# One streaming encoder step on one core: a root per token tile, token tiles first in the load queue, gate rows spread later, slot-weight sums in a gap

## The chip, the cores and the metric

The kernel runs on one core of a Trainium2 chip. The metric is the device time of one execution in microseconds, median of three runs. The core has five engines with a queue of instructions each: TensorE (PE, with its weight loads as PEld), VectorE (DVE), ScalarE (ACT), GpSimd (POOL) and SyncE (SP). Any of SP, ACT and POOL can issue DMA transfers. Engines wait for each other on semaphores.

## The reference

One layer of a hybrid encoder, for 512 prompt tokens and 8 x 16 sample tokens (640 tokens in all, width 1024):

```
mod = silu(c) @ w_ada + b_ada                        # shift, scale, gate; twice, per request
h   = rms_norm(x, norm1_g) * (1 + sc1) + sh1
q, k, v, indexer, stick-breaking q/k/v, gate logits = split(h @ w_in)
o_a = attention over the top-k keys that an indexer picks
o_b = stick-breaking attention (per-frame causal, in log space)
merged = sigmoid(gl_a) * (o_a @ w_branch_a) + sigmoid(gl_b) * (o_b @ w_branch_b)
x   = x + g1 * (merged @ w_out)
h   = rms_norm(x, norm2_g) * (1 + sc2) + sh2
x   = x + g2 * moe(h)      # 16 experts in 4 groups, top 2 of one group, weights normalised
```

All data are float32. New keys and values are outputs too.

## The kernel before, in words

Every engine's program is written out by hand, in order, with semaphores between them; nothing reorders it. The 640 tokens are five tiles of 128 (`NT`, the fifth holds the samples). SBUF is one tensor `mem` cut by hand.

Weights come in slabs of 2 MB through four rotating buffers. SP issues them in a fixed order (L646 to L663) and reuses a buffer when PE has counted `slab_used` up. The first slabs are ada 0, ada 2, the qa columns of `w_in`, and ada 1; near the merge they are the two halves of the gate columns, `w_branch_a` (two transfers), `w_branch_b`, and then two more gate halves (L663).

The head. SP issues eight small loads (condition vectors, `const_f` with the identity and eps, bias and norm rows, L635 to L643), then the five token tiles (L645), then slabs. ACT takes Silu of the conditions (L819), squares each token tile with a running sum (L831), and takes one root over the sums of all tiles (L833). PE turns the Silu result (L1602) and spreads the small rows (L1608 to L1614); VectorE copies these rows out (L1117 to L1120), waits for `h_sums`, takes one reciprocal (L1124), and then for each tile scales it (L1129) into one of two buffers `ht`; PE turns it (L1595), and ACT and VectorE each copy half of the result. ACT's squares have used the same two buffers `ht` as a place to write. After the fifth tile PE does the ada products (L1625) of slabs 0 and 2, the rows are turned (L1636), ACT and VectorE modulate, and PE starts the qa projection (L1677).

The merge. For 16 units PE makes two gate products (L1996) and two branch products (L2007), always two units' gates and then two units' branches. ACT takes sigmoids (L1039), VectorE multiplies (L1397), and POOL adds the two (L747). Ahead of its 16 additions POOL waits until the last attention unit is done (`bv_done`) and spreads the gate, shift and scale rows of the second half of the layer from a DRAM table over the partitions: two calls of `spread` (L742, L743), each one transfer for the prompt and eight for the samples. VectorE waits for them only in the residual (L1403).

Into the experts. VectorE computes the router's choice, ranks the 1280 token entries into slots of 64-row units, and gives PE one-hot matrices. PE multiplies them into slot tokens (L2081); VectorE turns these into row numbers (`slots_ready`, L1531), for which POOL waits to gather the first rows (L774). VectorE then sums each token's two affinities (L1533 to L1536), normalises them, and builds the matrix for PE's second product, the slot weights (L2088), which PE does before it turns the first gathered rows. The expert loop follows.

Of the kernel before, what the change touches and what calls it, by code (L numbers as in the profile page):

```python
# [29 lines left out]
ALU = mybir.AluOpType  # L30
ACT = mybir.ActivationFunctionType
X = mybir.AxisListType.X

P = 128
D = 1024
# [6 lines left out]
HD = 64  # L42
# [22 lines left out]
NCOND = 1 + DEC_B  # L65
# [12 lines left out]
O_CF = O_H + 5120  # L78
NCF = 5 * 128 + 16 + 16 + 2 * UNITS + 4 * NT + 4 + 16
# [4 lines left out]
O_TMP = O_ST + 180  # L84
# [54 lines left out]
def build(nc, a, o, scratch):  # L139

    ctx = ExitStack()
    with ctx:
# [6 lines left out]
        def view(at, n, pat=None, **dims):  # L149
            v = mem[:, at:at + n]  # L150
            return v if pat is None else v.rearrange(pat, **dims)
# [20 lines left out]
        xt = view(O_F, 5120, "p (t n) -> p t n", t=NT)  # L172
# [18 lines left out]
        eps = view(O_CF + 544 + UNITS, 1)  # L191
        at = O_CF + 545 + UNITS
# [18 lines left out]
        ssum = view(st, NT); rstd = view(st + 5, NT)  # L211
# [11 lines left out]
        rows_t = view(O_OB + 2 * P, P)  # L223
# [4 lines left out]
        s9T = view(O_OA + 1280 + 28 * P, KD * 32, "p (k n) -> p k n", k=KD)  # L228
        assert 1280 + 28 * P + KD * 32 <= 5120
        ht = [view(O_TMP + 1024 * i, 1024) for i in range(2)]  # L230
        c9 = view(O_TMP + 6144, 1024)[0:NCOND]
        s9 = view(O_TMP + 7168, 1024)[0:NCOND]

# [38 lines left out]
        g1 = {False: view(O_TMP, 1024), True: view(O_TMP + 1024, 1024)}  # L272
        bc2 = {False: view(O_TMP + 2048, 2048), True: view(O_TMP + 4096, 2048)}
# [28 lines left out]
        aw = [view(rt + 30 + 5 * i, 5) for i in range(2)]  # L302
        den = view(rt + 40, 5); rden = view(rt + 45, 5)
# [319 lines left out]
        def spread(eng, dst, lo, n, s, s_prompt=None):  # L623

            eng.dma_start(dst[False], modd[0:1, lo:lo + n].broadcast_to([P, n])).then_inc(s_prompt or s, 16)
            for b in range(DEC_B):
                eng.dma_start(dst[True][DEC_S * b:DEC_S * b + DEC_S, :],
                              modd[1 + b:2 + b, lo:lo + n].broadcast_to([DEC_S, n])).then_inc(s, 16)
# [3 lines left out]

        @block.sync
        def _(sp):
            sp.dma_start(c9[0:1, :], a["c_prompt"]).then_inc(c9_ld, 16)  # L635
            sp.dma_start(c9[1:NCOND, :], a["c_sample"]).then_inc(c9_ld, 16)
            sp.dma_start(view(O_CF, NCF), a["const_f"]).then_inc(c_ld, 16)
            for n_, at in (("b_ada", 0), ("norm1_g", 48), ("norm2_g", 56)):
                row = a[n_].rearrange("a (r n) -> (a r) n", n=P)
                sp.dma_start(rows_t[at:at + row.shape[0]], row).then_inc(rows_ld, 16)  # L640
            sp.wait_ge(rows_zero, 1)
            for i, n_ in enumerate(("qn_g", "kn_g")):
                sp.dma_start(rows_t[64 + i:65 + i, 0:HD], a[n_]).then_inc(rows_ld, 16)  # L643
            for t in range(NT):
                sp.dma_start(xt[:, t, :], xs if t == SMP else xp[P * t:P * t + P, :]).then_inc(tile_ld[t], 16)  # L645
            for n, s in enumerate(slabs):  # L646
                if n >= NSLAB:
                    sp.wait_ge(slab_used, n - NSLAB + 1)
                for dst, src in slab_moves(s, n):
                    sp.dma_start(dst, src).then_inc(slab_ld[n % NSLAB], 16)  # L650
                if s == ("b", XB - 1):

                    sp.wait_ge(av_done, NA)
                    for w, n_ in enumerate(("cache_b_k", "cache_b_v")):
                        sp.dma_start(xb[w], a[n_][0, XB].rearrange("(c p) h d -> p c (h d)", p=P)).then_inc(xb_ld, 16)
                if n == NSLAB:
                    sp.dma_start(view(O_CB, NCB // 2), a["const_b"]).then_inc(cb_ld, 16)
                if s == ("brb",):

                    sp.wait_ge(bv_done, NB)  # L660
                    sp.wait_ge(rows_st, 160)
                    for g in range(2):
                        sp.dma_start(gx[g], by_k(w_in, COL["gl"] + D * g + 512, 512)).then_inc(gx_ld[g], 16)  # L663

            def expert_part(e, w):

                k = 3 * (e % 3) + w
                src = a[("w_exp_gate", "w_exp_up", "w_exp_down")[w]][0, e].rearrange("(k p) n -> p k n", p=P)
                sp.dma_start(mw[k].rearrange("p (k n) -> p k n", k=4 if w == 2 else KD), src).then_inc(w_ld[k], 16)


            sp.wait_ge(merge_read, 1)
            for w in range(3):
                expert_part(0, w)
            expert_part(1, 0)
            sp.wait_ge(wo_done, 1)
            expert_part(1, 1)
            expert_part(1, 2)
            expert_part(2, 0)
            sp.wait_ge(e_in, 1)  # L680
            expert_part(2, 1)
            sp.wait_ge(slots_ready, 1)
            sp.wait_ge(h2_st[0], 48)
            sp.wait_ge(h2_st[1], 32)
            sp.wait_ge(hx_ld, 16)
            sp.wait_ge(unit_w_ready, 1)
            expert_part(2, 2)
            for e in range(3, NE):
                for w, part_used in enumerate((gate_used, up_used, down_used)):
                    sp.wait_ge(part_used, e - 2)  # L690
                    expert_part(e, w)

            sp.wait_ge(y_all, 1)
            for t in range(NT):
                sp.dma_start(ysum[t], yd[P * t:P * t + P, :]).then_inc(tile_ld[t], 16)
            for t in range(NT):
                sp.wait_ge(e_out, 100 + t + 1)
                sp.dma_start(out_rows("y", t), ysum[t]).then_inc(out_st, 16)
            sp.wait_ge(out_st, 16 * NT)
# [3 lines left out]
        def _(pool):  # L703
            own = Own(pool, pool_did)
# [12 lines left out]
            for t in range(NT):  # L717
                pool.wait_ge(ro_ready, t + 1)
                if t == 0:
                    pool.wait_ge(zeros_ready, 1)  # L720
                    for r_ in range(0, TOK + UNIT, P):
                        n_ = min(P, TOK + UNIT - r_)
# [16 lines left out]
            pool.wait_ge(m9_st[1], 64)  # L739

            pool.wait_ge(bv_done, NB)
            spread(pool, g1, 2048, 1024, bc2_ld)  # L742
            spread(pool, bc2, 3072, 2048, bc2_ld)  # L743
            for i in range(16):
                m, h = i // 2, i % 2
                pool.wait_ge(gb_ready, i + 1)
                g.tensor_tensor(mergedT[:, m, 320 * h:320 * h + 320], gb[i % 2][0], gb[i % 2][1],  # L747
                                ALU.add).then_inc(merged, 1)
            pool.wait_ge(merge_read, 1)
# [31 lines left out]
            for e in range(NE):  # L781
                n = g.value_load(unit_n[0:1, e:e + 1], min_val=1, max_val=TOK // UNIT)
                at = g.value_load(unit_0[0:1, e:e + 1], min_val=0, max_val=UNITS - 1)
# [20 lines left out]
        def _(act):  # L804
            own = Own(act, act_did)
            s = nc.scalar
# [6 lines left out]
            def copy_out(key, dst, src=None, scale=1.0):  # L813
                r = result(act, key)
                ins = s.activation(dst, r if src is None else src, ACT.Copy, scale=scale)
                return ins

            act.wait_ge(c9_ld, 32)
            s.activation(s9, c9, ACT.Silu).then_inc(s9_ready, 1)  # L819
            act.wait_ge(c_ld, 16)  # L820
# [7 lines left out]

            for t in range(NT):
                act.wait_ge(tile_ld[t], 16)  # L830
                own(s.activation(ht[t % 2], xt[:, t, :], ACT.Square, accum_out=ssum[:, t:t + 1]))  # L831
                own.settle()
            s.activation(rstd, ssum, ACT.Sqrt, scale=1.0 / D, bias=eps).then_inc(h_sums, 1)  # L833
            for t in range(NT):
                r = result(act, ("h1T", t, 0))
                read(("h1T", t, 0), s.activation(hT[:, 0:4, P * t:P * t + P],
# [15 lines left out]
            for t in range(NT):  # L852
                r = result(act, ("qa", t))
                read(("qa", t), s.activation(tok[:, t, 0:512], r, ACT.Copy))
            for t in range(NT):
                r = result(act, ("kvq", t))
# [242 lines left out]
        def _(dve):  # L1099
# [3 lines left out]
            def step(ins):  # L1103
                own(ins)
                own.settle()
# [14 lines left out]
            own(v.tensor_copy(g9, r[:, 2 * P:4 * P].rearrange("p (i n) -> p i n", i=2)))  # L1120
            own.settle()
            dve.sem_inc(free[place["rows"][0]], 1)
            dve.wait_ge(h_sums, 1)
            step(v.reciprocal(rstd, rstd))  # L1124
            for t in range(NT + 1):
                if t < NT:
                    if t >= 2:
                        result(dve, ("h1T", t - 2, 1))
                    v.tensor_scalar(ht[t % 2], xt[:, t, :], rstd[:, t:t + 1], None, ALU.mult).then_inc(h_ready, 1)  # L1129
                if t >= 1:  # L1130
                    r = result(dve, ("h1T", t - 1, 1))
                    read(("h1T", t - 1, 1), v.tensor_copy(hT[:, 4:8, P * (t - 1):P * t], r.rearrange("p (k q) -> p k q", k=4)))
# [385 lines left out]
            own(v.tensor_tensor(at_pos_b, bcast(iota_p, [P, 2 * NT, P], 1), bcast(entry_pos, [P, 2 * NT, P], 2), ALU.is_equal))  # L1518
            own.settle()
            dve.sem_inc(entries_ready, 1)  # L1520

            r = result(dve, "slots")[:, 0:3 * UNITS].rearrange("p (a j) -> p a j", a=3)
            own(v.memset(ids[:, UNITS:UNITS + 2, :], 0))
# [6 lines left out]
            step(v.tensor_scalar(ids[:, 0:UNITS, 1], dest, -1.0, row_half, ALU.mult, ALU.add))  # L1530
            dve.sem_inc(slots_ready, 1)  # L1531

            for i, oh in enumerate((oh1, oh2)):  # L1533
                step(v.tensor_tensor(t2, aff, oh, ALU.mult))
                step(v.tensor_reduce(aw[i], t2, X, ALU.add))
            step(v.tensor_tensor(den, aw[0], aw[1], ALU.add))  # L1536
            step(v.reciprocal(rden, den))
            for i in range(2):
                own(v.tensor_tensor(ew[:, :, i], aw[i], rden, ALU.mult))
# [640 lines left out]
```

## Time and profile before

| | |
|---|---|
| median of 3 runs | 1188.93 us (1186.75 to 1189.68) |
| profiled execution | 1187.63 us, its span 1185.8 us |
| PE busy | 1068.2 us, 90% of the span |
| VectorE, ACT, POOL busy | 389.4, 244.0, 143.5 us |
| mean granted clock of PE | 0.96 of full speed |
| DMA | 217.05 MB, mean 183 GB/s |

The span is the time from the first to the last instruction of one execution; the rest of the execution's time lies around it. The chain of waits is followed back from the last instruction: each piece is what released the next. A wait of an engine off that chain costs nothing. The granted clock is a share of 2.4 GHz; 0.50 is the lower level.

### The profile page before, as it was taken

Reading aid. Unit: us, or ns where it says so; the run is one execution under the profiler, and the core shown is the slowest. Engines: PE = TensorE matmul, PEld = TensorE weight load, DVE = VectorE, ACT = ScalarE, POOL = GpSimd, SP = SyncE. Lnnn points to the kernel's source line nnn. Section 1 sums busy time; section 2 is a strip of 40 time slices with the busy share of each in tenths; the row PEclk is TensorE's granted clock in tenths of the full one; section 3 lists DMA queues with packets and bytes.
Section 4 is the critical chain, followed back from the end, with each engine's and each line's share of the span. In section 5 each row is a group of like instructions: output and inputs, shape, how many; then the busy total and the mean of one; then the engine's idle time right before and its main releaser. Section 6 shows DMA issues by size and latency. Waiting matters only on the chain.

```text
span 1185.8 us, 21577 instructions
## 1 busy us (share of the span) xinstructions
PE 1068.2 (90%) x8635; PEld 714.0 (60%) x8635; DVE 389.4 (33%) x894; ACT 244.0 (21%) x486; POOL 143.5 (12%) x218
## 2 busy tenths in 40 slices
PE   5899999989979979889999999955999999999991
PEld 4445764456745757667677754425676767677770
DVE  2100738956777655200000003353111111111114
ACT  4111232127745335200000001121111101010100
POOL 0000210110000000200000010010222222222221
PEclk9999999999979989999999999976999999999996
DMA  9542855345000248880030027066796996999935
GB/s 344 221 149 88 311 170 189 110 122 193 1 1 1 72 144 283 231 232 1 19 123 1 1 99 293 36 220 223 256 305 204 358 366 215 316 381 373 382 93 195
DMA packets 103029, 217.05 MB, mean 183 GB/s; under 512 B 9477, under 2 KB 17749, under 8 KB 102694
## 3 DMA queue, kind: packets, MB, share of 16 engines
q1 hardware_dynamic: 91446, 184.42, 43.5%
q0 software_dynamic: 11504, 31.52, 9.8%
q8 instruction: 55, 0.90, 0.3%
q14 instruction: 24, 0.20, 0.1%
HBM read 196.87 MB, written 19.05 MB: 182 GB/s over the span
## 4 chain that ended last, share of the span: by engine, by line
PE 79%; DVE 8%; DMA 5%; ACT 4%; issue 3%; SPq 0%; DVEq 0%; POOL 0%; ACTq 0%; POOLq 0%
PE ps L2105 17%; PE ps L1996 10%; PE ps L1651 10%; PE ps L2116 9%; PE ps L2007 6%; PE ps L2051 4%; PE ps L1677 3%; PE ps L1696 3%; PE ps L1595 3%; PE ps L1625 2%; DMA mem<-in_w_branch_b 2%; DMA mem<-in_x_sample 2%; PE ps L1778 2%; PE ps L2110 1%; ACT mem L952 1%
## 5 line engine op out<-in xcount | busy, mean ns | idle before, releaser
L2105 PEld LDWEIGHTS ps<-mem 128*64 128x64 f32 x3584 | 198.5, 138 | 24.8 <-issue 21.4
L2105 PE MATMUL ps<-mem 128*64 128x128 f32 x3584 | 209.5, 275 | 2.1 <-DVE mem L1552 0.9
L1996 PE MATMUL ps<-mem 128*128 128x320 f32 x512 | 139.2, 433 | 1.1 <-DVEq L1359 1.1
L1996 PEld LDWEIGHTS ps<-mem 128*128 128x128 f32 x512 | 97.3, 190 | 41.5 <-issue 1.3
L1651 PE MATMUL ps<-mem 128*128 128x512 f32 (+1 forms) x320 | 113.3, 514 | 1.8 <-ACT mem L912 0.9
L2116 PE MATMUL ps<-mem 128*64 128x512 f32 x448 | 107.1, 597 | 4.2 <-DVE mem L1566 0.5
L1651 PEld LDWEIGHTS ps<-mem 128*128 128x128 f32 x320 | 54.2, 191 | 58.5 <-issue 58.5
L1595 PE MATMUL ps<-mem 128*128 128x128 f32 x432 | 66.9, 294 | 22.8 <-DVE mem L1129 8.8
L1397 DVE TENSOR_TENSOR mem<-mem,ps 128x320 f32<-128x320 f32 x32 | 15.6, 488 | 198.1 <-PE ps L2007 198.1
L1564 DVE TENSOR_TENSOR mem<-mem,ps 128x128 f32<-128x128 f32 x56 | 16.1, 288 | 186.9 <-PE ps L2105 186.9
L1595 PEld LDWEIGHTS ps<-mem 128*128 128x128 f32 x432 | 53.4, 151 | 36.7 <-DVE mem L1129 9.8
L2007 PE MATMUL ps<-mem 128*128 128x320 f32 x256 | 72.2, 441 | 3.5 <-DMA mem<-in_w_branch_b 3.4
L2051 PE MATMUL ps<-mem 128*128 128x512 f32 x160 | 72.3, 608 | 2.1 <-POOL mem L747 2.1
L2007 PEld LDWEIGHTS ps<-mem 128*128 128x128 f32 x256 | 49.5, 194 | 25.1 <-DMA mem<-in_w_branch_b 3.9
L1093 ACT ACTIVATE mem<-ps,mem 128x512 f32<-128x512 f32 x28 | 19.2, 687 | 185.5 <-PE ps L2116 185.5
L2116 PEld LDWEIGHTS ps<-mem 128*64 128x64 f32 x448 | 31.2, 136 | 40.4 <-issue 40.4
L2051 PEld LDWEIGHTS ps<-mem 128*128 128x128 f32 x160 | 30.4, 194 | 38.7 <-issue 38.7
L1039 ACT ACTIVATE mem<-ps 128x320 f32<-128x320 f32 x32 | 14.0, 437 | 191.1 <-PE ps L1996 191.1
L1566 DVE COPY mem<-ps 128x128 f32<-128x128 f32 x56 | 16.3, 292 | 95.2 <-PE ps L2110 95.2
L791 POOL DMA_INDIRECT expert_rows<-mem x28 | 44.6, 1595 | 23.3 <-POOL mem L789 23.3
L1214 DVE MAX8 mem<-mem 128x8 f32<-128x644 f32 (+3 forms) x65 | 41.0, 631 | 2.0
L1215 DVE MATCH_REPLACE8 mem<-mem 128x644 f32<-128x644 f32 (+3 forms) x65 | 39.9, 613 | 0.0
(288 smaller groups left out, 1141.3 us busy)
## 6 DMA issues: line engine op xcount, KB each, us to landing
mem<-in_w_exp_gate SPq DMA_DIRECT2D x16, 2048.0 KB, 12.5
mem<-in_w_exp_up SPq DMA_DIRECT2D x16, 2048.0 KB, 17.9
mem<-in_w_exp_down SPq DMA_DIRECT2D x16, 2048.0 KB, 22.3
mem<-in_w_ada SPq DMA_DIRECT2D x12, 2048.0 KB, 14.4
mem<-in_w_in SPq DMA_DIRECT2D x9, 2048.0 KB, 13.1
mem<-in_cache_b_k SPq DMA_DIRECT2D x8, 1024.0 KB, 5.6
mem<-in_cache_b_v SPq DMA_DIRECT2D x8, 1024.0 KB, 8.5
mem<-in_w_out SPq DMA_DIRECT2D x2, 2048.0 KB, 11.4
```

Source lines behind the costliest of these rows:

```text
L791: pool.indirect_dma_start(y_halves, bass.IndirectOffsetOnAxis(ap=idx_out, axis=0), yj, None, compute_op=ALU.add).then_inc(y_st, 16)
L1214: step(v.max(top8, sc))
L1215: step(v.match_replace(sc, top8, sc, TAKEN))
L1595: last = tr(dst[:, P * k:P * k + P], b, ident)
L1651: last = mm(b[:, 0:w], hT[:, k, P * t:P * t + P], slab_k[n][:, k, 0:w], start=(k == 0), stop=(k == KD - 1))
L1677: last = mm(b, hT[:, k, P * t:P * t + P], slab_k[n_qa][:, k, :], start=(k == 0), stop=(k == KD - 1))
L1696: last = mm(b[:, 0:320], slab_k[n][:, k, P * m:P * m + P], hT[:, k, 320 * h:320 * h + 320], start=(k == 0), stop=(k == KD - 1))
L1996: last = mm(b[:, 0:320], w[:, k, P * (m % 4):P * (m % 4) + P], hT[:, k, 320 * h:320 * h + 320], start=(k == 0), stop=(k == KD - 1))
L2007: last = mm(b[:, 0:320], slab_4[slab_no[s_] % NSLAB][:, k, P * m:P * m + P], rows_of[:, k, 320 * h:320 * h + 320], start=(k == 0), stop=(k ...
L2051: last = mm(b, mergedT[:, k, P * t:P * t + P], slab_k[sn][:, k, :], start=(k == 0), stop=(k == KD - 1))
L2105: last = mm(b[UNIT * h:UNIT * h + UNIT, 0:P], x_, w[:, k, 256 * h + P * c:256 * h + P * c + P], start=(k == 0), stop=(k == KD - 1), skip_g ...
L2116: last = mm(bank(7)[UNIT * n:UNIT * n + UNIT, :], hidT[c][:, UNIT * h:UNIT * h + UNIT], w[:, 2 * h + c, 512 * n:512 * n + 512], start=(c = ...
```

## The change

Four edits. (1) The eight small loads move from SP's queue to the beginning of ACT's; the token tiles are now SP's first issues. (2) The norm's root and reciprocal are done for each tile by itself, and the squares go to two buffers of their own. (3) POOL issues the two `spread` calls inside its addition loop, after the second unit's products are ready and ahead of the second addition. (4) The five VectorE instructions that sum the slot weights move ahead of VectorE's wait for PE's slot product.

```diff
@@ first norm's buffers
         ht = [view(O_TMP + 1024 * i, 1024) for i in range(2)]
+        sq_first = [view(O_TMP + 2048 + 1024 * i, 1024) for i in range(2)]
@@ SP
-            sp.dma_start(c9[0:1, :], a["c_prompt"]).then_inc(c9_ld, 16)
-            sp.dma_start(c9[1:NCOND, :], a["c_sample"]).then_inc(c9_ld, 16)
-            sp.dma_start(view(O_CF, NCF), a["const_f"]).then_inc(c_ld, 16)
-            for n_, at in (("b_ada", 0), ("norm1_g", 48), ("norm2_g", 56)):
-                row = a[n_].rearrange("a (r n) -> (a r) n", n=P)
-                sp.dma_start(rows_t[at:at + row.shape[0]], row).then_inc(rows_ld, 16)
-            sp.wait_ge(rows_zero, 1)
-            for i, n_ in enumerate(("qn_g", "kn_g")):
-                sp.dma_start(rows_t[64 + i:65 + i, 0:HD], a[n_]).then_inc(rows_ld, 16)
             for t in range(NT):
                 sp.dma_start(xt[:, t, :], ...).then_inc(tile_ld[t], 16)
@@ POOL
             pool.wait_ge(bv_done, NB)
-            spread(pool, g1, 2048, 1024, bc2_ld)
-            spread(pool, bc2, 3072, 2048, bc2_ld)
             for i in range(16):
                 m, h = i // 2, i % 2
                 pool.wait_ge(gb_ready, i + 1)
+                if i == 1:
+                    spread(pool, g1, 2048, 1024, bc2_ld)
+                    spread(pool, bc2, 3072, 2048, bc2_ld)
                 g.tensor_tensor(mergedT[:, m, 320 * h:320 * h + 320], gb[i % 2][0], gb[i % 2][1],
                                 ALU.add).then_inc(merged, 1)
@@ ACT
+            (the eight loads and the wait for rows_zero, as they stood on SP, now act.dma_start)
             act.wait_ge(c9_ld, 32)
             s.activation(s9, c9, ACT.Silu).then_inc(s9_ready, 1)
...
             for t in range(NT):
                 act.wait_ge(tile_ld[t], 16)
-                own(s.activation(ht[t % 2], xt[:, t, :], ACT.Square, accum_out=ssum[:, t:t + 1]))
+                own(s.activation(sq_first[t % 2], xt[:, t, :], ACT.Square, accum_out=ssum[:, t:t + 1]))
                 own.settle()
-            s.activation(rstd, ssum, ACT.Sqrt, scale=1.0 / D, bias=eps).then_inc(h_sums, 1)
+                s.activation(rstd[:, t:t + 1], ssum[:, t:t + 1], ACT.Sqrt, scale=1.0 / D, bias=eps).then_inc(h_sums, 1)
@@ VectorE, first norm
-            dve.wait_ge(h_sums, 1)
-            step(v.reciprocal(rstd, rstd))
             for t in range(NT + 1):
                 if t < NT:
+                    dve.wait_ge(h_sums, t + 1)
+                    step(v.reciprocal(rstd[:, t:t + 1], rstd[:, t:t + 1]))
                     if t >= 2:
                         result(dve, ("h1T", t - 2, 1))
@@ VectorE, slots
             dve.sem_inc(entries_ready, 1)
+            for i, oh in enumerate((oh1, oh2)):
+                step(v.tensor_tensor(t2, aff, oh, ALU.mult))
+                step(v.tensor_reduce(aw[i], t2, X, ALU.add))
+            step(v.tensor_tensor(den, aw[0], aw[1], ALU.add))
 
             r = result(dve, "slots")[:, 0:3 * UNITS].rearrange("p (a j) -> p a j", a=3)
...
             dve.sem_inc(slots_ready, 1)
 
-            for i, oh in enumerate((oh1, oh2)):
-                step(v.tensor_tensor(t2, aff, oh, ALU.mult))
-                step(v.tensor_reduce(aw[i], t2, X, ALU.add))
-            step(v.tensor_tensor(den, aw[0], aw[1], ALU.add))
             step(v.reciprocal(rden, den))
```

## Rows read from the trace of the kernel before

**Rows 1.** The page: engines' shares of the chain that ended last.

```profile
PE 79%; DVE 8%; DMA 5%; ACT 4%; issue 3%; SPq 0%; DVEq 0%; POOL 0%; ACTq 0%; POOLq 0%
```

**Rows 2.** Timeline of the merge's beginning: start, us, engine, line, operation, [idle before].

```profile
482.94 1.37 SPq L650 DMA_DIRECT2D mem<-in_w_branch_a  x2
...
512.17 8.42 PE L2007 MATMUL ps<-mem 128*128 128x320 f32 x24 [3.36 <-DMA mem<-in_w_branch_b]
```

**Rows 3.** Chain of waits in the merge: start, us, what.

```profile
487.33 24.80 DMA mem<-in_w_branch_b
...
615.73 8.61 PE ps L2007 x32
```

**Rows 4.** Transfers by line: branch A (L650), the spread (L627), one gate half alone.

```profile
DMA to landing us min/median/max: 8.5/10.9/13.2
...
L627 POOL DMA_DIRECT2D mem<-mod_rows x16: 484/486/547, 488.4 to 496.2; - x16
...
DMA to landing us min/median/max: 11.0/16.1/23.6
...
DMA to landing us min/median/max: 8.8/8.8/8.8
```

**Rows 5.** Timeline of the head, columns as in rows 2.

```profile
0.74 1.28 ACT L819 ACT_TABLE_LOAD   x1 [0.74 <-PEq L2166]
...
3.03 1.05 ACT L819 ACTIVATE mem<-mem 9x1024 f32<-9x1024 f32 x1 [1.01 <-DMA mem<-in_c_sample]
...
3.64 1.93 SPq L645 DMA_DIRECT2D mem<-in_x_prompt  x4
5.04 1.02 PE L1602 MATMUL ps<-mem 9*128 9x9 f32 x8 [5.04 <-DMA mem<-in_const_f]
...
8.51 1.06 ACT L831 ACTIVATE mem<-mem 128x1024 f32<-128x1024 f32 x1 [4.42 <-DMA mem<-in_x_prompt]
...
10.05 0.42 DVE L1120 COPY mem<-ps 128x256 f32<-128x256 f32 x1
...
16.39 0.19 DVE L1124 RECIPROCAL mem<-mem 128x5 f32<-128x5 f32 x1 [5.92 <-ACT mem L833]
```

**Rows 6.** Chain of waits in the head, columns as in rows 3.

```profile
24.89 2.15 PE ps L1625 x72
...
27.33 2.21 PE ps L1625 x72
...
33.81 8.80 PE ps L1677 x16
...
44.72 7.06 PE ps L1677 x16
```

**Rows 7.** Two slab loads of the head: durations in ns, start, and landing.

```profile
L650 SPq DMA_DIRECT2D mem<-in_w_ada x1: 3157/3157/3157, 7.0 to 7.0; - x1
L650 SPq DMA_DIRECT2D mem<-in_w_in x1: 5126/5126/5126, 10.2 to 10.2; - x1
...
DMA to landing us min/median/max: 17.3/19.2/21.0
```

**Rows 8.** Windows: us, engines' busy time, PE's granted clock, DMA share, GB/s.

```profile
1.50:6.50 5.00, 1.02 (x8) 0.92 (x8) 0.23 (x1) 1.58 (x2) 1.50 (x2) 1.00 0.80 261
...
512.10:516.60 4.50, 4.42 (x10) 2.93 (x11) 0.45 (x1) 0.00 (x0) 0.00 (x0) 0.62 1.07 165
```

**Rows 9.** Timeline on the way into the experts, columns as in rows 2.

```profile
809.72 0.19 DVE L1524 COPY mem<-ps 128x36 f32<-128x36 f32 x1 [1.24 <-issue]
...
811.23 0.25 DVE L1534 TENSOR_TENSOR mem<-mem 128x80 f32<-128x80 f32 x1
...
812.53 0.19 DVE L1537 RECIPROCAL mem<-mem 128x5 f32<-128x5 f32 x1
...
813.67 4.48 PE L2088 MATMUL ps<-mem 128*128 128x36 f32 x20 [4.00 <-DVEq L1543]
```

**Rows 10.** SP's own waits from 780 to 820: line, releaser, us, times, longest.

```profile
SPq L686 <- DVE mem L1545: 2.6, 1, 2.6
```

More of the change, by code:

```diff
@@ L816, in copy_out @@
                 return ins
+            act.dma_start(c9[0:1, :], a["c_prompt"]).then_inc(c9_ld, 16)
+            act.dma_start(c9[1:NCOND, :], a["c_sample"]).then_inc(c9_ld, 16)
+            act.dma_start(view(O_CF, NCF), a["const_f"]).then_inc(c_ld, 16)
+            for n_, at in (("b_ada", 0), ("norm1_g", 48), ("norm2_g", 56)):
+                row = a[n_].rearrange("a (r n) -> (a r) n", n=P)
+                act.dma_start(rows_t[at:at + row.shape[0]], row).then_inc(rows_ld, 16)
+            act.wait_ge(rows_zero, 1)
+            for i, n_ in enumerate(("qn_g", "kn_g")):
+                act.dma_start(rows_t[64 + i:65 + i, 0:HD], a[n_]).then_inc(rows_ld, 16)
             act.wait_ge(c9_ld, 32)
```

## The prediction

> **What bounds the kernel now.** I read the page first, then the chain of waits over the whole span, then timelines, waits and landings of the three stretches that the change touches. The chain lies on PE for 79% of the span [rows 1], so a stage before or between PE's work is worth exactly what PE waits there, and what PE then loses at half clock. SP's slab loads, POOL's row stores and the later stages are started by PE's progress, so time won early is carried to the end unless a transfer is late in its turn.
>
> Stretch one, the head. PE's main work begins with the qa projection at 33.81 us [rows 6]. It hangs on: token tiles landed, one root for all five, a reciprocal at 16.39, five scale-and-transpose rounds that end at 24.89, two ada slabs on PE (the second from 27.33), modulation [rows 5, 6]. Stretch two, the merge. After branch A's first eight products PE stands 3.36 us, until 512.17, for branch B's weights, which landed 24.80 us after their issue at 487.33 [rows 2, 3]; when it goes on, the granted clock is 0.62 over 4.5 us [rows 8], which is mostly the lower of the two levels (1.2 against 2.4 GHz). Stretch three, the way into the experts: PE waits 4.00 us for VectorE before the slot-weight product at 813.67, and VectorE itself had stood 1.24 us just before 809.72 [rows 9].
>
> **The change part by part.**
>
> *Gate rows later (merge).* POOL issues 18 transfers, two large ones and sixteen small ones that start 488.4 to 496.2, 0.49 us each; together they are about 3.1 MB by their shapes, and they landed 11.0 to 23.6 us after issue [rows 4]. So they lie exactly beside SP's branch weights. Without them the queue holds branch A (2 MB, second half landed by 482.94 + 1.37 + 13.2 = 497.5 at the latest, though part of that was beside the spread [rows 2, 4]) and branch B behind it. A 2 MB slab issued with nothing beside it landed in 8.8 us [rows 4], so branch B lands by 497.5 + 8.8 = 506.3. PE wants it at 512.17 - 3.36 = 508.8. Lower bound of the gain 0 (B as late as now), upper bound the whole wait, 3.36; I take all of it. Then the clock: after the wait 24 products took 8.42 us, where a full set of 32 takes 8.61 [rows 3], that is 6.46 for 24; 1.96 us were lost at the low level. With no wait ahead of it I count that back too (bounds 0 and 1.96). Sum -5.3 us.
> What the move adds: POOL now waits for the second gated product, issues the 18 (18 x 0.49, about 9 us) and only then makes its second addition. Queued behind it: VectorE's fourth gated product waits for that addition. But PE first makes gates 2 and 3, 64 products, twice the 32 of [rows 3] and so some 17 us, so about 8 us are spare. The spread lands some 25 us after 516, while the rows are read after the merge, near 718; SP asks for no slab in that time except the gate halves, issued before. Cost 0; if POOL took over 17 us, each further one would show as PE waiting in the fourth branch product.
>
> *Sums of the slot weights.* Five small VectorE instructions, 811.23 to 812.53 = 1.30 us [rows 9], leave the path ahead of weights_ready and go into the 1.24 us in which VectorE waits for PE's slot product. They overrun it by about 0.15 us (settling included), which delays slots_ready by as much. Gain 1.30 - 0.15 = 1.15 us, with 0.9 and 1.3 as bounds. What is late next: the gather of the first expert rows, which would be 0.15 us later; SP, which waits for it and then for the slot weights, still waited 2.6 us for the latter [rows 10], so after 1.15 + 0.15 us it is still 1.3 us early. PE's 4.5 us product stays last. -1.15 us.
>
> *Head.* First the constants. Eight small issues go from SP to ACT. ACT issued none before, so their price there is not shown: on SP they are what lies between the engines' first instructions at 0.74 and the first tile at 3.64, 2.9 us in all [rows 5]; POOL's cost 0.49 to 0.55 each [rows 4], which would make 4 to 4.4. I take SP's, as the same kind of queue. The table load (1.28, at 0.74 until now hidden) and the Silu (1.05) come behind them: Silu ends at 3.64 + 1.28 + 1.05 = 5.97 instead of 4.08. const_f is issued as early as before, but beside the tiles: I take 6.0 us for PE's first transposes instead of 5.04 [rows 5] (bounds 5.97 from Silu, and 13.5, when all five tiles had landed until now). VectorE's row copies ended at 10.05 + 0.42 = 10.47, 5.43 after that start; now 11.4.
> Then the norm. VectorE no longer waits for the root of all tiles (till 16.39) and starts at 11.4. From 16.39 to 24.89 it and PE took 8.50 us for five rounds with one reciprocal; four more at 0.22 make 9.4, so the transposes end at 20.8, 4.1 us earlier. ACT hides behind that: Square from about 6.0 (tile 0, 2.9 us earlier than the 8.51 shown, is there), 1.15 each, then a table load 1.28 once (taken from the norm's single one) and a root a tile. Even at 1 us each, which is far above the 0.19 of the reciprocal of the same size, the roots end at about 9.4, 11.6, 13.7, 15.9 and 18.0, and VectorE asks for them at 11.4, 12.4, 15.2, 17 and 18.7. Without that cover each us by which ACT is late goes into the sum. The squares go to a buffer of their own, so the scaled tiles are not waited for.
> Then the slabs, which decide how much of the 4.1 arrives. The second ada slab landed 7.0 + 17.3 = 24.3, qa's 10.2 + 21.0 = 31.2 [rows 7]. SP's issues come 2.9 us earlier, but the bytes ahead of them are the same, moved from one queue to another, and the DMA engines were already busy 0.80 of the time from 1.5 to 6.5 [rows 8]: only 1 us of idle to be won, of which part is the start. I take 0.7: 23.6 and 30.5. PE comes to the second ada at 20.8 + 2.5 = 23.3, starts at 23.6, and by the 6.48 us from 27.33 to 33.81 would begin qa at 30.1; the slab holds it till about 30.4. Gain 3.4 us; bounds 2.6 (slabs no earlier) and 4.1 (slabs never wait).
> A rule of the Trainium skill bears on this: DMA: Bandwidth & Descriptors, section "Issuing engines are not separate DMA queues", says that transfers started by different engines run on the same 16 DMA engines and interleave, so that several issuers save only the issue time. The trace agrees: POOL's and SP's transfers of [rows 3, 4] lay beside each other and took up to 24.80 us each. By the rule the head gives 3.4; if queues were independent, 4.1.
> Clock in the head: qa's first sixteen products took 8.80 us where the next sixteen took 7.06 [rows 6], so 1.7 us are lost after PE's pause before 33.81. That pause stays, a little longer, and I leave the loss as it is; bounds -1.7 (it goes) and +1.7 (it doubles).
>
> **Sum.** 3.4 + 5.3 + 1.15 = 9.85 us. The profiled execution took 1187.63 us (span 1185.8 and 1.8 around it): 1177.8. The median of the three runs shown lies 1.3 above it; half of that added gives 1178.5 for the time after.
>
> **Rivals.**
> *The head gives nothing, or costs a little.* The constants on ACT's queue reach PE later than 6.0: the transposes end 14.8 us after const_f (6.0 to 20.8), so from a landing at 10.1 on nothing of the root's gain is left, and at 12 the head costs 1.9. For it: the tiles now have the first places, and const_f is the only large piece among the constants. Against it: POOL's first transfer, issued behind SP's branch slabs and gate halves, landed in 11.0 us [rows 4], so two queues do share. Total 1181 to 1183.
> *Constants starve behind everything SP has queued.* This is the one that ends slower. If const_f came only after the tiles and the two ada slabs, at 23.6, transposes would end at 38.4, 13.5 later than now; against 6.45 won elsewhere that is +7: 1194 to 1195. It decides from a landing at 16.6 on. What speaks for it is only that branch B took 24.80 us beside another queue; that was half the rate, not starvation.
> *The merge wait stays.* If branch A's odd layout and not the spread is what delays branch B, or if it is the gate halves behind it, only the head and the tail count: 1187.63 - 4.55 + 0.65 = 1183.7. Against: both queues were full from 488 to 512, and 3.1 MB of that were the spread's.
> *More than the sum.* The head's low-clock stretch goes as well, or the slabs never hold PE: 1176 to 1177, both 1174 to 1175.
>
> **How the numbers follow.** Forecast (7 to 12 us won, own range 1175.5 to 1182) 0.70; head without gain 0.14; merge wait stays 0.06; starving 0.03; more than 12 us won 0.07. The range 1174.5 to 1184 takes the forecast and the cases without head or merge gain. What a measurement here can tell from no change is about 0.3%, 3.6 us: faster 0.93 (nearly all of the first three and the last), same 0.04 (two rivals at once), slower 0.03.
>
> **What would show it.** Right: no wait of PE for branch B near 505 and no stretch at 0.62 there; branch B landing within 20 us of issue; POOL's 18 issues near 510 and no PE wait at the fourth branch product; VectorE's first scale near 12, transposes ended near 21, the qa products starting near 30.4 with the qa slab as the last to come; VectorE busy through the slot product, and PE's wait before the slot weights 2.9 us instead of 4.00. Wrong: PE's first transposes after 10 us; a second table load among the roots; a new low-clock stretch; the same span between 34 and 487 of before not found again.

## The result, and the profile after

The changed kernel took 1183.04 us (median of 5 runs, 1180.37 to 1183.4) against 1188.06 for the kernel before: measured ratio 0.9945, 95% interval 0.9927 to 0.9964 (it is not the quotient of the two medians, 0.9958). A second set, the fifth run below, gave 1180.4 us, 0.9935 (0.992 to 0.995). The profiled execution took 1183.28 us, its span 1181.5. So it is faster by 5 to 8 us where 9.85 were forecast, and the time lies inside the range, 4.5 us above the point.

**The head won next to nothing.** Timeline of the head after; ACTq and SPq are issues of transfers.

```profile
0.74 0.53 ACTq L811 DMA_DIRECT2D mem<-in_c_prompt  x1
0.74 1.81 SPq L637 DMA_DIRECT2D mem<-in_x_prompt  x4
...
1.63 0.38 ACTq L813 DMA_DIRECT2D mem<-in_const_f  x1
...
3.89 0.32 ACTq L819 DMA_DIRECT2D mem<-in_kn_g  x1
4.24 1.28 ACT L821 ACT_TABLE_LOAD   x1 [4.24 <-issue]
5.53 1.05 ACT L821 ACTIVATE mem<-mem 9x1024 f32<-9x1024 f32 x1
...
9.34 1.06 ACT L833 ACTIVATE mem<-mem 128x1024 f32<-128x1024 f32 x1 [2.75 <-DMA mem<-in_const_f]
9.36 1.02 PE L1604 MATMUL ps<-mem 9*128 9x9 f32 x8 [9.36 <-DMA mem<-in_const_f]
...
11.01 0.45 PE L1610 MATMUL ps<-mem 128*128 128x128 f32 x1 [0.64 <-DMA mem<-in_kn_g]
...
15.08 0.16 DVE L1128 RECIPROCAL mem<-mem 128x1 f32<-128x1 f32 x1
```

const_f was issued at 1.63, hardly later than before (1.49), but PE had it only at 9.36 instead of 5.04 [rows 5]; the last small row held PE until 11.01. VectorE's copies of those rows ended at 14.9 instead of 10.47, so that its first reciprocal came at 15.08 and its first scale at 15.28. The rest is in the chain of waits:

```profile
3.89 6.99 DMA mem<-in_kn_g
...
24.33 2.15 PE ps L1627 x72
26.47 0.29 issue
26.76 2.21 PE ps L1627 x72
...
33.24 9.69 PE ps L1679 x16
...
45.03 7.06 PE ps L1679 x16
```

Transposes end at 24.33 instead of 24.89, qa begins at 33.24 instead of 33.81 [rows 6]: 0.57 us won. Its first sixteen products took 9.69 us instead of 8.80, since the low level of the clock began ahead of them this time (0.50 already from 32 to 33 us, where the kernel before has 1.00). So at qa's second half the kernel is 0.3 us behind.

**The merge won what was forecast.** Chain of waits, then the landing of branch B (issued at 487.28) and of the spread's sixteen small transfers, then the window that answers to the second of [rows 8].

```profile
489.31 17.47 PE ps L1998 x64
506.77 8.61 PE ps L2009 x32
515.38 17.23 PE ps L1998 x64
```

```profile
DMA to landing us min/median/max: 14.7/14.7/14.7
...
L628 POOL DMA_DIRECT2D mem<-mod_rows x16: 484/484/544, 516.9 to 524.7; - x16
DMA to landing us min/median/max: 2.4/4.5/8.4
```

```profile
512.10:516.60 4.50, 4.50 (x19) 3.15 (x18) 0.98 (x2) 0.00 (x0) 0.92 (x2) 1.00 0.02 5
```

The first 32 branch products run through in 8.61 us at the higher level. Branch B landed 14.7 us after issue, not 24.80 [rows 3], 4.8 us before these products began. From the first gate product to the end of these branches it is 26.07 us. Before it was 31.39, from 489.20 in the timeline to 520.59 in the chain:

```profile
489.20 17.47 PE L1996 MATMUL ps<-mem 128*128 128x320 f32 x64 [1.14 <-DVEq L1359]
...
520.59 17.23 PE ps L1996 x64
```

So 5.3 us, all of it still there when the next pair of units is done: POOL's nine microseconds of issues, from 516, held nobody. By themselves the spread's sixteen small transfers land within 2.4 to 8.4 us; beside SP's they took 11.0 to 23.6 [rows 4].

**The sums won what was forecast.** Timeline on the way into the experts, and SP's own wait:

```profile
804.29 0.24 DVE L1524 TENSOR_TENSOR mem<-mem 128x80 f32<-128x80 f32 x1
...
805.60 0.19 DVE L1530 COPY mem<-ps 128x36 f32<-128x36 f32 x1
...
807.10 0.19 DVE L1539 RECIPROCAL mem<-mem 128x5 f32<-128x5 f32 x1
...
808.25 4.48 PE L2090 MATMUL ps<-mem 128*128 128x36 f32 x20 [2.91 <-DVEq L1545]
```

```profile
SPq L678 <- DVE mem L1547: 1.3, 1, 1.3
```

PE waits 2.91 instead of 4.00 [rows 9], and SP's spare time behind the gather is the 1.3 us that was worked out from [rows 10].

**Two losses between them are in no step of the change.** The residual's load took 15.14 us where it had taken 14.29 (0.85), and the first expert's 96 products 8.17 instead of 7.20 (0.97):

```profile
698.99 15.14 DMA mem<-in_x_sample
...
808.25 4.48 PE ps L2090 x20
...
814.50 8.17 PE ps L2107 x96
```

Head +0.3 (0.57 won, 0.89 to the clock), merge -5.3, sums -1.1, these two +1.8: -4.3, the difference of the spans. The experiments below say which of these are chance.

### The profile page after: what moved, and what is told of

It is laid out like the page before. It is cut to its first block, busy times and chain, and to the rows that moved or that the text cites. A ratio compares the mean times of both kernels' runs of the same rounds, so it can differ in the third digit from the quotient of the medians.

```text
span 1181.5 us, 21581 instructions
## 1 busy us (share of the span) xinstructions
PE 1066.0 (90%) x8630; PEld 713.7 (60%) x8635; DVE 390.2 (33%) x898; ACT 244.7 (21%) x490; POOL 143.6 (12%) x218
## 4 chain that ended last, share of the span: by engine, by line
PE 81%; DVE 8%; ACT 4%; issue 3%; DMA 3%; ACTq 0%; DVEq 0%; POOL 0%; POOLq 0%
PE ps L2107 17%; PE ps L1998 12%; PE ps L1653 10%; PE ps L2118 9%; PE ps L2009 6%; PE ps L2053 4%; PE ps L1679 3%; PE ps L1698 3%; PE ps L1597 3%; PE ps L1627 2%; PE ps L1780 2%; DMA mem<-in_x_sample 1%; PE ps L2112 1%; ACT mem L954 1%; PE ps L1771 1%
## 5 line engine op out<-in xcount | busy, mean ns | idle before, releaser
L1566 DVE TENSOR_TENSOR mem<-mem,ps 128x128 f32<-128x128 f32 x56 | 16.1, 288 | 187.7 <-PE ps L2107 187.7
L740 POOL TENSOR_TENSOR mem<-mem 128x320 f32<-128x320 f32 x16 | 13.7, 858 | 403.5 <-DVEq L1402 403.4
```

## The experiments

The fourth is an edit of the kernel before, the fifth is the changed kernel itself, all others are edits of the changed kernel; each was timed beside the kernel before. Medians of 6 runs (third and fourth: 12, tenth: 5).

**First: constants back on SP, the norm per tile kept.**

```diff
 SP:  +(the eight loads, ahead of the tiles)
 ACT: -(the eight loads)
```

> The changed kernel with the eight constant loads back on SP, ahead of the token tiles. Theory A (the constants on ACT's queue come in behind the tiles, const_f at 9.36 us and the last norm row at 10.9, and that holds the whole head): PE's first transposes again near 5.0 us, VectorE's row copies done near 10.5, the first scale near 11.5, tile transposes ended near 21 instead of 24.3, and qa's products from about 31.2, when their slab lands: 2.0 us earlier than in the changed kernel, some 1181 us, or up to 1 us off that by the clock. Rival B (the reciprocal and the root for each tile are what make the five rounds slow): transposes end at 24 or later, as the tiles come 2.9 us later, and the time is that of the changed kernel or 1 to 2 us above it.

1179.41 us, 0.9913 (0.9895 to 0.9931). PE timeline:

```profile
4.43 1.02 PE L1604 MATMUL ps<-mem 9*128 9x9 f32 x8 [4.43 <-DMA mem<-in_const_f]
...
19.46 2.17 PE L1627 MATMUL ps<-mem 128*32 128x128 f32 x72
...
25.92 4.07 PE L1627 MATMUL ps<-mem 128*32 128x128 f32 x72 [4.29 <-DMA mem<-in_w_ada]
...
34.30 8.16 PE L1679 MATMUL ps<-mem 128*128 128x512 f32 x15 [3.37 <-DVE mem L1151]
```

Rival B falls: with one root and one reciprocal for each tile the transposes are done at 19.5, 5.4 us earlier than in the kernel before. But the gain is gone at the next step: PE stands 4.29 us for the second ada slab, then works at half clock (4.07 us for what takes 2.17), and qa begins at 34.30, no earlier than ever, where 31.2 was expected: this wait had no place in the expectation. The time seemed 3 us below that of the changed kernel, which this profile does not explain; the fifth and sixth runs settle it.

**Second: const_f alone first on SP.**

```diff
 SP:  +sp.dma_start(view(O_CF, NCF), a["const_f"]).then_inc(c_ld, 16)     # ahead of the tiles
 ACT: -act.dma_start(view(O_CF, NCF), a["const_f"]).then_inc(c_ld, 16)
```

> The changed kernel with const_f alone moved from ACT's queue to the first place in SP's; the seven small loads stay on ACT. Theory A: const_f lands near 4.5, the Silu ends near 6.2, PE's first transposes start at about 6.2 instead of 9.36, the small rows no longer stand behind const_f in their queue, transposes end near 21.2, qa's products start near 29.8: 3.4 us under the changed kernel, about 1179.6 us. Rival A2 (not const_f but any load on ACT's queue is late beside SP's tiles, for its place in the queue and not its size): the last norm row is still near 10 us, PE's row products stay near 11, and nothing is won.

1178.32 us, 0.9904 (0.9887 to 0.9921). What PE waited for up to 32 us, and its chain:

```profile
PE ps L1604 <- ACT mem L821: 5.9, 1, 5.9
...
PE ps L1610 <- DMA mem<-in_kn_g: 1.7, 1, 1.7
```

```profile
4.30 19.40 DMA mem<-in_w_ada
23.75 2.21 PE ps L1627 x72
...
30.23 8.74 PE ps L1679 x16
```

const_f landed 3.5 us after its issue, PE starts at 5.9 behind the Silu, and qa begins at 30.23, 3.0 us earlier than in the changed kernel and 0.4 from what was expected. Theory A holds in the trace, with a share for the second rival: the last small row still came 5.4 us after its issue (at 8.5), and PE stood 1.7 us for it. What ends last in this profile is the second ada slab, at 23.7; in the ninth run, the same kernel, it is the last small row. The time is 0.3% to 0.4% under the two sets of the changed kernel, as forecast, though its interval still meets that of the second set (0.992 to 0.995).

**Third: the spread early again.**

```diff
             pool.wait_ge(bv_done, NB)
+            spread(pool, g1, 2048, 1024, bc2_ld)
+            spread(pool, bc2, 3072, 2048, bc2_ld)
```

> The changed kernel with the two spreads of gate rows back ahead of POOL's additions. Theory A: the wait of PE for branch B's weights (3.4 us) and the stretch at half clock behind it (2.0 us) come back, 5.3 us above the changed kernel, about 1188.3 us; PE's merge begins and ends as before the change. Rival C (the merge is held by the gate halves or by branch A's layout, and the gain came from elsewhere): the wait stays away and the time that of the changed kernel.

1188.73 us, 0.9988 (0.9972 to 1.0005). The wait is back (first fence, PE's waits), and the stretch at half clock behind it (second, a window):

```profile
PE ps L2008 <- DMA mem<-in_w_branch_b: 5.2, 1, 5.2
```

```profile
512.20:516.70 4.50, 4.50 (x9) 2.93 (x10) 0.00 (x0) 0.00 (x0) 0.00 (x0) 0.50 0.99 166
```

The merge is worth 0.43% to 0.53% against the two sets of the changed kernel, 5 to 6 us, and rival C falls. The wait is longer than the 3.36 us of before: PE came to its first gate product 1.9 us earlier here (487.35 against 489.20), while branch B landed at 512.15 against 512.13. What PE had won ahead of the merge was lost in the wait, so this run does not say what the head is worth.

**Fourth: the queue move alone, on the kernel before.**

> The kernel before with only the eight loads moved from SP's to ACT's queue; one root for all tiles, spread and sums as before. Theory A: const_f again near 9.4 us, ACT, which needs its eps, starts its squares near 9.4 instead of 8.5, the root ends near 17.3 instead of 16.4, transposes end near 25.8, qa's products start about 0.9 us later than before: 1189 us, no gain at all from tiles that land 3 us earlier. Rival B: the tiles' earlier landing is worth 1 to 3 us by itself, 1185 to 1187.

1190.19 us, 1.0006 (0.9993 to 1.002). PE's timeline, and its chain:

```profile
9.57 1.02 PE L1602 MATMUL ps<-mem 9*128 9x9 f32 x8 [9.57 <-DMA mem<-in_const_f]
...
34.49 8.80 PE ps L1677 x16
```

const_f reached PE at 9.57, qa began at 34.49, 0.7 us later than in the kernel before; in time no change can be told. Tiles that land 1.3 to 3.6 us earlier are worth nothing by themselves.

**Fifth and sixth: the changed kernel and the first experiment's, side by side.**

> The changed kernel itself once more, on the same chip as the next three, to compare with. Theory A (the head of the changed kernel is worth nothing, the merge 5 us, the slot-weight sums 1 us): 0.9945 of the time before, some 1183 us, const_f again at 9.3 to 9.6 us. Its wait for the last load of the residual and its low-clock stretches are read a second time: if the 0.85 us by which that load took longer and the longer low-clock stretch of the first expert belong to the change, both are seen again; if they are chance, one or both are not.

> The same kernel as the first experiment (eight constant loads back on SP, ahead of the tiles). There the transposes ended at 19.5, but PE then waited 4.3 us for the second ada slab, which landed at 25.8, and did its products at half clock, so that qa began at 34.3, no earlier than in any other kernel. Theory A': the norm's gain is spent at that slab, the wait is seen again, and the time is within 1.5 us of the changed kernel's run beside it. Rival: the profile of the first experiment was an unlucky one, PE's wait is under 2 us here, and the time is 3 us under the changed kernel, as the medians of different sets of runs had it.

1180.4 us, 0.9935 (0.992 to 0.995), and 1179.92 us, 0.9926 (0.9909 to 0.9943): no difference. In the sixth, PE's wait for the slab was seen again, 2.80 us, and qa began at 32.02:

```profile
24.28 3.19 PE L1627 MATMUL ps<-mem 128*32 128x128 f32 x72 [2.80 <-DMA mem<-in_w_ada]
```

In the fifth const_f came at 9.40 and qa at 33.23, as in the first profile. Constants first make the slabs late, tiles first make the constants late: two heads of nearly one length. The 3 us of the first experiment were chance between sets of runs. The residual's load took 14.6 to 15.5 us in all the later profiles, in the fourth too (15.35), which has none of edits 2 to 4, and in the first and sixth (14.61 and 15.02), which have not edit 1: no edit goes with its 0.85 us. The first expert's products took 7.41 us in the fifth and 6.7 to 8.4 elsewhere: chance too.

**Seventh: the sums late again.**

```diff
             dve.sem_inc(entries_ready, 1)
-            (the five sums)
...
             dve.sem_inc(slots_ready, 1)
+            (the five sums)
```

> The changed kernel with the five slot-weight sums back behind slots_ready. Theory A: PE's wait before the slot-weight product is 4.0 us again instead of 2.9, the product begins 1.1 us later against the router's end, and the time is 1.1 us above the changed kernel, which five rounds may just not tell apart. Rival: the wait grows but the time does not, since the gather or the clock's next rise sets when the first expert's products run at speed.

1183.07 us, 0.9952 (0.9939 to 0.9965), against 0.9935 beside it. PE's wait is 4.01 again:

```profile
PE ps L2090 <- DVEq L1545: 4.0, 1, 4.0
```

The trace shows the 1.1 us; the times differ by 2.7 us the same way, but their intervals overlap, so by time the edit is not shown.

**Eighth, ninth and tenth: PE kept busy in its pause ahead of qa.** On the second experiment's kernel; the ninth is that kernel unchanged, the eighth has seven added products, the tenth three.

```diff
             turn_mod(0)
+            b = may_fill(("qa", 0))
+            for _ in range(3):
+                mm(b, ident, view(O_CF, 512), start=True, stop=True)
             n_qa = slab_wait(("in", "qa"))
```

> The second experiment's kernel (const_f first on SP) with seven products added that PE does while it waits for modulation ahead of qa; their result is overwritten and used by nothing. Theory D (the head's loss at half clock comes from PE's pause before qa): the clock does not fall, qa's first sixteen products take about 7.1 instead of 8.74 us, 1.7 us under the second experiment's kernel. Rival: the clock falls all the same, or the added products delay qa's first by up to 0.5 us, and the time is the same or slightly more.

> The second experiment's kernel again (the changed kernel, const_f first on SP), as a control on the chip of the next two. Theory A: qa from about 30.2 us as before, held by the second ada slab, and its first sixteen products take 8.7 to 9.7 us; 0.9905 of the time before, some 1178 us.

> The same kernel with three added products instead of seven in PE's pause ahead of qa (seven took 6.2 us and delayed qa by 2.7, which ate the 1.7 that the clock gave back). Theory D: three take 2.6 us, less than the pause of 3.4, qa still begins near 30.2 and its first sixteen take near 7.1: 1.7 us under the control. Rival: the rest of the pause is enough for the clock to fall, and the time is the control's.

1179.61, 1179.78 and 1175.51 us; 0.9926 (0.9913 to 0.9939), 0.9903 (0.988 to 0.9927) and 0.9873 (0.9853 to 0.9893). Window of the control, then of the kernel with three:

```profile
28.00:40.00 12.00, 9.38 (x16) 3.89 (x16) 2.30 (x4) 1.19 (x2) 0.00 (x0) 0.72 1.05 390
```

```profile
28.00:40.00 12.00, 11.20 (x94) 5.48 (x92) 2.30 (x4) 1.52 (x2) 0.00 (x0) 1.00 1.05 390
```

The chain has qa's first sixteen products, in the control and with three:

```profile
30.62 9.62 PE ps L1679 x16
```

```profile
30.96 7.11 PE ps L1682 x16
```

The mean clock of that stretch is 0.72 without and 1.00 with the added work; qa's first sixteen products take 7.11 us instead of 9.62 (8.74 in the second experiment's profile of the control's kernel). The loss at half clock comes from the pause ahead of it, as theory D says. Seven products were my mistake in size: each took 0.88 us, they delayed qa by 2.7 us and ate the gain. With three the times are 4 us apart, of which the trace explains 2.5; the two intervals overlap (0.988 to 0.9927 and 0.9853 to 0.9893), so the effect on the clock is shown, while the gain in time only points the same way.

One expectation of the ninth missed: the second ada slab did not hold qa. Its chain runs over the last small row, which ACT issued at 3.13 and which landed 5.26 us later; qa began at 30.62 instead of 30.23. With const_f first on SP, the rows left on ACT's queue are the next to be late.

**Eleventh: the router's pauses too.** The tenth kernel, with 4, 7, 6 and 2 more such products in PE's pauses between the second norm's last turn and the slot weights.

> The kernel of three added products with nineteen more on PE in its four pauses of the router, from the last turn of the second norm to the slot weights; results unused. In the changed kernel that stretch stands at half clock for some 38 us; the slot-weight product takes 4.48 us there and the first expert's 96 products 7.2 to 8.2 where later ones take 5.2 to 5.5. Theory D: the clock stays up, the slot weights take about 2.3, the first expert's products 5.3, the turns and logits at the end of the norm some 1 us less, 4 to 6 us under the kernel of three. Rival: the clock falls all the same or the added products at half clock overrun the pauses, each by up to 5 us, and the time is above.

1173.51 us, 0.9862 (0.9842 to 0.9883): the fastest of all, though not apart from the tenth by its interval. PE there:

```profile
802.18 2.58 PE L2104 MATMUL ps<-mem 128*128 128x36 f32 x20 [0.18 <-DVEq L1546]
806.16 1.09 PE L1598 MATMUL ps<-mem 128*128 128x128 f32 x4 [1.41 <-DMA mem<-h_rows,mem]
808.13 7.71 PE L2121 MATMUL ps<-mem 128*64 128x128 f32 x96 [0.88 <-DVE mem L1555]
```

The slot weights took 2.58 us instead of 4.48, but then the gather of the first rows is late, PE waits 1.41 us for it, the clock falls, and the first expert's products are as slow as ever (7.71). Part of the expected gain only. This profile is of the slowest of the six executions, 1177.28 us; what went otherwise in one near the median, 3.8 us faster, no trace shows.

## Why the prediction was right or wrong

The sum was 3.4 + 5.3 + 1.15. Two terms hold and one fails, so the total came out at half to four fifths. That the time lies inside the range is no merit of the sum: the range took in the case of a head without gain.

*Merge, 5.3.* Right in mechanism and size: 5.3 in the trace, 5 to 6 by the third experiment. The bound for branch B's landing, 506.3, was generous: it landed at 502.0. The rival "the merge wait stays" falls.

*Sums, 1.15.* Right in the trace: 1.09, with the late gather, the 1.3 us left to SP and PE's product as the last to come, as worked out. By time it is not shown (seventh experiment).

*Head, 3.4.* Wrong, 0.57 measured, and the step that failed is one line: "I take 6.0 us for PE's first transposes instead of 5.04". It was 9.36. I had the bounds right (5.97 to 13.5) and took the value at the low end, with no row for it: that two queues share the DMA engines is said further on, but no price is drawn from it. The landings after show what sharing did: the first two tiles landed at 4.5 and 6.2, the third at 9.6, and in the 3.4 us between, a table that POOL loads (in_rotary, 8.6) and const_f (9.34) came in, some 1.25 MB together with that tile. The bytes of the queues agree: until 4 us SP's had moved 0.64 MB and ACT's 0.01; from 5 to 8 us ACT's moved 0.35 of 1.18 MB. So a load of 0.39 MB, issued 0.9 us after the first tile's, came behind most of two tiles and then moved at a share of the rate: 7.7 us instead of 3.5. The nearest row was there: the quickest of POOL's small spread transfers took 11.0 us beside SP's queue [rows 4]; alone they take 2.4 to 8.4, as the profile after shows. I read it as proof of sharing and not as a price, and as POOL's first transfer, which took 10.7 and is one of the two large ones. The second and fourth experiments show that this is the step: const_f moved to the front of SP's queue gives 2.6 to 3.0 us back at qa's start (ninth and second run), and the queue move by itself costs 0.7 there. Of the signs named, those of the merge and the sums came (POOL's issues at 516 instead of 510); those of the head did not: first scale at 15.28 for 12, transposes ended at 24.33 for 21, qa at 33.24 for 30.4.

The rest of the head's working held. "The transposes end 14.8 us after const_f" gives 24.2 for 9.36; they ended at 24.33. The first rival's reckoning, nothing left from a landing at 10.1 on, came close: 9.36 left 0.6. So that rival, with its 1181 to 1183 and a chance of 0.14, was the case. The limit by the slabs was real as well: the first experiment ended its transposes at 19.5, stood for the second ada slab and won nothing. In the changed kernel the slabs came 1.4 (second ada, 22.9) and 2.9 us (qa, 28.3) earlier, not 0.7, and nobody was there to use it. ACT's issues cost 3.5 us for eight, not 2.9; const_f's lateness hid that. The root for each tile was off the path, with one table load, at 0.29 us each.

*Clock in the head.* Left as it was in the sum, with 1.7 either way. It took 0.89 us more in the first profile and nothing more in the second of the same kernel. The rival "more than the sum" is added up too low for both cases together: 1177.8 less 1.7 and 0.7 is 1175.4, not 1174 to 1175.

## What to carry to other kernels

Moving loads to another engine's queue does not make them cheaper, it changes who goes first: what the first instruction needs belongs ahead of the bulk in one queue, and a small load issued beside megabytes took two to four times as long here (const_f 7.7 us for 3.5, the spread's small transfers 16.1 for 4.5 at the median). Before an order of loads is changed, every consumer of the loads that become late is followed, and the landing of the next slab, since the gain goes no further than that. A short pause of PE cost half to three quarters of its length again at half clock behind it (1.7 to 2.6 us for 3.4): where it can't be removed, some products without use inside it gave that back in the trace here.

## What the runs showed of the hardware

The granted clock fell around PE's pauses of some 3.4 us, not always at the same moment: ahead of qa it stood at 0.50 already inside the pause in the first profile of the changed kernel (32 to 33 us), while in the second it was 1.00 there and 0.50 from 34 to 35, when qa had begun. Products added in the pause kept it at 1.00 (0.72 without, as means from 28 to 40 us). How much of the work behind a pause ran at the lower level differed between executions of one kernel (qa's first sixteen products took 9.69 and 8.80 us in these two profiles), which may be part of the 3 us by which runs of one kernel differ; that was not tested.
